# A hybrid encoder layer on one core: the skip product and the addition of the backward direction move from the vector engine to GpSimd in the forward SSM scan

## The chip, the cores and the metric

The kernel runs on one NeuronCore of one Trainium2 chip. The metric is the device time of one execution in microseconds (us), the median of several runs. TensorE is written PE, the vector engine DVE, the scalar engine ACT, GpSimd POOL, and the engine that issues most DMAs SP.

## The reference

One encoder layer on two request groups of 1024 and 256 tokens, in float32. A joint input projection feeds windowed attention, a bidirectional state-space scan (SSM) and attention to memory tokens; an output projection and a gated feed-forward part follow. The change lies in the SSM alone:

```
def ssd_bidirectional(z, xbc, dt_raw, conv_w, conv_b, dt_bias, a_log, d_skip, norm_w):
    ...
    y_f = ssd_scan(xs, dt[:, :, 0], a_neg[0], bm, cm)
    y_b = ssd_scan(xs[:, ::-1], dt[:, ::-1, 1], a_neg[1], bm[:, ::-1], cm[:, ::-1])[:, ::-1]
    y = y_f + y_b + d_skip.astype(jnp.float32)[:, None] * xs.astype(jnp.float32)
    y = y.reshape(b, s, SSM_INNER) * jax.nn.silu(z.astype(jnp.float32))
    return rms_norm(y, norm_w).astype(z.dtype)
```

The skip product is `d_skip * xs`; the addition of the backward direction is `+ y_b`.

## The kernel before

The program is a row of stages, each with a loop of its own per engine: norm, projections, the backward scan, the forward scan (`ssm_forward`), attention, memory attention, output projection, feed-forward. Engines meet at the end of each stage.

`ssm_backward` leaves, in the SBUF buffer `y_back`, the part of the backward direction that comes from the chunks behind. `ssm_forward` then goes through ten tiles of 128 tokens (t = 0 to 7 for the long sequence, 8 and 9 for the short one; the scan state is set to zero anew before tile 8). Each engine runs its own instruction list in order, and the lists meet through counting semaphores (`wait_ge`). In tile t:

- PE turns x and B of the tile (`x_ps`, `m_ps`), multiplies C by the state (`y_ps`), makes C·B (`m_ps`), then does 32 small matmuls (16 calls, each in two passes) for the tile before (`within(t-1)`, into `g_ps`, L1629), then the state update (`s_ps`) and the turning back of tile t-2.
- ACT copies `b_tok` and `x_tok` out of PSUM (L1747, L1748), makes the decay factors `drop` in two halves of eight small activations (L1758) and an exponential (L1764), squares the result of tile t-1 between the second half and its exponential (`squares`, L1727), and stores tile t-2.
- POOL multiplies `x_tok` by the step sizes into `x_dt` (two instructions, L1710), which it may overwrite only when `g_ps` of t-1 is finished (semaphore `diag`); then `mse` and `rstd` of tile t-1 (L1698, L1703).
- DVE copies `acs_t` (L1803), which ACT's factors wait for, makes `x_dec` (L1807), takes `y` out of PSUM (L1815), makes the skip product in `y2` (L1819), masks C·B (L1826, two instructions), adds `y_back` to `y2` (L1830), scales the state (L1834), adds `y2` to `y` (L1837), then gates tile t-1 (`gate`: L1786 adds `g_ps`, L1789 multiplies by z), updates the state (L1842), makes `m_t` from the factors (L1848, two instructions) and normalises tile t-1 (L1796), which waits for `rstd`.

In the profile's rows the buffer `y2` is shown as `sf_y`. The loop that PE waits in is closed like this: `within` of tile t-1 ends, DVE gates t-1, ACT squares it and, after its exponential, copies `b_tok` of the next tile, and only then PE goes on to C·B and to `within` of the next tile.

Of the kernel before, what the change touches and what calls it, by code (L numbers as in the profile page):

```python
# [1517 lines left out]
def ssm_forward(nc, proj, xbc_c, acs_rows, ident_dram, small, R, mix_t):  # L1518
# [6 lines left out]
    with ExitStack() as ctx:  # L1525
# [31 lines left out]
        g_ps = b.ps("sf_gps", [P, NS, PS])  # L1557
        t_ps = b.ps("sf_tps", [P, 4, P])
        S = {n: b.sem(f"sf_s_{n}") for n in (
            "const", "half", "turn", "xcopy", "bcopy", "xd", "off", "st", "h", "zero", "cb", "cbm", "acs", "drop", "e", "m", "diag", "y", "gated", "sq", "pow", "yn", "tn", "tcopy", "xdt")}  # L1560
        loaded, z_loaded, rows_loaded = b.sems("sf_l", 2), b.sems("sf_zl", 2), b.sems("sf_rl", 2)
        stored = b.sem("sf_stored")
        block = b.block()
# [16 lines left out]
        def before(t, n):  # L1580

            return isinstance(t, int) and t < n
# [32 lines left out]
        @block.tensor  # L1615
        def _(pe):
            T = nc.tensor
            pe.wait_ge(S["const"], 48)

            def within(t, first=False):  # L1620

                pe.wait_ge(S["xdt"], 2 * t + 2)
                pe.wait_ge(S["m"], 2 * t + 2)
                if not first:

                    pe.wait_ge(S["gated"], 2 * t - 1)
                for h in range(NS):
                    for d in range(2):
                        m = T.matmul(g_ps[:, h], m_t[:, d, h], x_dt[:, d, h], start=(d == 0), stop=(d == 1))  # L1629
                m.then_inc(S["diag"], 1)  # L1630

            def turn_back(t, s, first=False):
                pe.wait_ge(S["yn"], t + 1)
                if not first:
                    pe.wait_ge(S["tcopy"], t)
                for c in range(4):
                    m = T.transpose(t_ps[:, c], yn[:, s, c * P:(c + 1) * P], ident[:, :])
                m.then_inc(S["tn"], 1)

            def body(t, s):  # L1640
                first = before(t, 1)
                pe.wait_ge(loaded[s], loaded_value(t, s))
                if not first:

                    pe.wait_ge(S["xcopy"], t)
                    pe.wait_ge(S["bcopy"], t)
                    pe.wait_ge(S["cbm"], 2 * t)
                for c in range(4):
                    T.transpose(x_ps[:, 2 * c:2 * c + 2], xc[:, s, c * P:(c + 1) * P], ident[:, :])
                for g in range(NG):  # L1650
                    m = T.transpose(m_ps[:, g], xc[:, s, (4 + g) * P:(5 + g) * P], ident[:, :])
                m.then_inc(S["turn"], 1)

                if first:
                    pe.wait_ge(S["zero"], 1)
                else:
                    pe.wait_ge(S["h"], 2 * t)
                    pe.wait_ge(S["y"], 4 * t - 3)
                for g in range(NG):
                    m = T.matmul(y_ps[:, 4 * g:4 * g + 4], xc[:, s, (6 + g) * P:(7 + g) * P],  # L1660
                                 state[:, 4 * g:4 * g + 4], start=True, stop=True)
                m.then_inc(S["off"], 1)

                pe.wait_ge(S["bcopy"], t + 1)
                for g in range(NG):
                    m = T.matmul(m_ps[:, 2 + g], xc[:, s, (4 + g) * P:(5 + g) * P],
                                 xc[:, s, (6 + g) * P:(7 + g) * P], start=True, stop=True)
                m.then_inc(S["cb"], 1)
                if not first:
                    within(t - 1, before(t, 2))  # L1670
                pe.wait_ge(S["xd"], t + 1)
                for g in range(NG):
                    m = T.matmul(s_ps[:, 4 * g:4 * g + 4], b_tok[:, g], x_dec[:, 4 * g:4 * g + 4],
                                 start=True, stop=True)
                m.then_inc(S["st"], 1)
                if not before(t, 2):
                    turn_back(t - 2, s, before(t, 3))

            def reset(k):
                if k:  # L1680
                    pe.wait_ge(S["zero"], 2)

            order(pe, body, reset)
            within(NT - 1)
            turn_back(NT - 2, 0)
            turn_back(NT - 1, 1)

        @block.gpsimd
        def _(pool):
            b.clear_previous(pool)  # L1690
            g = nc.gpsimd
            g.memset(half[:, :], -0.5).then_inc(S["half"], 1)
            g.memset(eps[:, :], EPS).then_inc(S["half"], 1)
            pool.wait_ge(S["half"], 2)

            def rstd_of(t, first=False):
                pool.wait_ge(S["sq"], t + 1)
                g.tensor_tensor(mse[:, :], ms[:, :], eps[:, :], ALU.add).then_inc(S["pow"], 1)  # L1698
                pool.wait_ge(S["pow"], 2 * t + 1)
                if not first:  # L1700

                    pool.wait_ge(S["yn"], t)
                g.tensor_tensor(rstd[:, :], mse[:, :], half[:, :], ALU.pow).then_inc(S["pow"], 1)  # L1703

            def body(t, s):
                pool.wait_ge(S["xcopy"], t + 1)
                for d in range(2):
                    if not before(t, 1):
                        pool.wait_ge(S["diag"], t)
                    g.tensor_tensor(x_dt[:, d], x_tok[:, :, :], bc(row(dt, t, d * NS, (d + 1) * NS), [P, NS, PS]),  # L1710
                                    ALU.mult).then_inc(S["xdt"], 1)
                if not before(t, 1):
                    rstd_of(t - 1, before(t, 2))

            order(pool, body)
            rstd_of(NT - 1)

        @block.scalar
        def _(act):
# [19 lines left out]
            def body(t, s):  # L1739
                act.wait_ge(S["turn"], t + 1)  # L1740
                if not before(t, 1):
                    act.wait_ge(S["st"], t)

                    act.wait_ge(S["y"], 4 * t - 2)
                    act.wait_ge(S["xdt"], 2 * t)
                    act.wait_ge(S["xd"], t)
                a.activation(b_tok[:, :, :], m_ps[:, 0:2], ACT.Copy).then_inc(S["bcopy"], 1)  # L1747
                a.activation(x_tok[:, :, :], x_ps[:, :, :], ACT.Copy).then_inc(S["xcopy"], 1)  # L1748


                act.wait_ge(S["acs"], t + 1)
                for d in range(2):
                    if d == 0:
                        act.wait_ge(rows_loaded[s], loaded_value(t, s))
                    if not before(t, 1):
                        act.wait_ge(S["m"], 2 * t - 1 + d)
                    for h in range(NS):
                        m = a.activation(drop[:, d, h], rows[:, s, d, h], ACT.Relu, scale=-1.0,  # L1758
                                         bias=acs_t[:, s, d * NS + h:d * NS + h + 1])
                    m.then_inc(S["drop"], 1)  # L1760
                    if d == 1 and not before(t, 1):
                        squares(t - 1, 1 - s, before(t, 2))
                    act.wait_ge(S["drop"], 2 * t + d + 1)
                    a.activation(drop[:, d], drop[:, d], ACT.Exp, scale=-1.0).then_inc(S["e"], 1)  # L1764
                if not before(t, 2):
                    store(t - 2, before(t, 3))
# [8 lines left out]
        def _(dve):  # L1775
# [3 lines left out]
            def hp(ap):  # L1779
                return ap.rearrange("p (h q) -> p h q", q=PS)  # L1780

            def gate(t, s):

                dve.wait_ge(S["diag"], t + 1)
                dve.wait_ge(S["y"], 4 * t + 4)
                v.tensor_tensor(hp(y[:, s]), hp(y[:, s]), g_ps[:, :, :], ALU.add).then_inc(S["gated"], 1)  # L1786
                dve.wait_ge(S["gated"], 2 * t + 1)
                dve.wait_ge(z_loaded[s], loaded_value(t, s))
# [10 lines left out]
            def body(t, s):  # L1799
# [11 lines left out]
                if not before(t, 2):  # L1811
# [2 lines left out]
                    dve.wait_ge(S["yn"], t - 1)  # L1814
                v.tensor_tensor(hp(y[:, s]), y_ps[:, :, :], bc(row(e_acs, t, 0, NS), [P, NS, PS]),  # L1815
                                ALU.mult).then_inc(S["y"], 1)
                if not before(t, 1):
                    dve.wait_ge(S["y"], 4 * t)
                v.tensor_tensor(hp(y2[:, :]), x_tok[:, :, :], bc(dsk[:, :].unsqueeze(2), [P, NS, PS]),  # L1819
                                ALU.mult).then_inc(S["y"], 1)  # L1820

                dve.wait_ge(S["cb"], t + 1)
                if not before(t, 1):
# [1 line left out]
                for d in range(2):  # L1825
                    v.tensor_tensor(cb[:, d, :, 0], m_ps[:, 2:4], bc(tri[:, d:d + 1, :], [P, NG, P]),  # L1826
                                    ALU.mult).then_inc(S["cbm"], 1)
                dve.wait_ge(S["y"], 4 * t + 2)
                yb = y_back[:, t] if isinstance(t, int) else y_back[:, ds(t, 1)].rearrange("p o n -> p (o n)")
                v.tensor_tensor(y2[:, :], y2[:, :], yb, ALU.add).then_inc(S["y"], 1)  # L1830

                if not before(t, 1):
                    dve.wait_ge(S["h"], 2 * t)
                v.tensor_tensor(scaled[:, :, :], state[:, :, :], bc(row(e_tot, t, 0, NS), [P, NS, PS]),  # L1834
                                ALU.mult).then_inc(S["h"], 1)
                dve.wait_ge(S["y"], 4 * t + 3)
                v.tensor_tensor(y[:, s], y[:, s], y2[:, :], ALU.add).then_inc(S["y"], 1)  # L1837
                if not before(t, 1):
                    gate(t - 1, 1 - s)
# [679 lines left out]
```

## Time and profile before

| | us |
|---|---|
| median of 3 runs (lowest to highest) | 2209.69 (2207.54 to 2212.36) |
| the profiled execution, its own time | 2212.37 |
| its span, first to last instruction | 2210.6 |
| the forward scan, about 551 to 690 of the span | 139 |

The profiled execution is 2.7 us above the median, inside the spread of the runs. The forward scan is 6% of the span. In its rows, times are counted from the start of the span; a DVE row's length includes the tail that overlaps the next instruction, so that what an instruction costs its queue is the distance between two starts. "[idle before <- releaser]" stands behind an instruction whose engine sat idle before it.

### The profile page before, as it was taken

What the parts mean: (1) busy time and instruction counts of PE and PEld (TensorE: products, weight loads), DVE (VectorE), ACT (ScalarE), POOL (GpSimd) and SP (SyncE); (2) the same over time, 40 slices, a digit from 0 to 9 for tenths busy, and PEclk for the clock granted to TensorE, in tenths of its full rate; (3) what the DMA queues carried; (4) which work ended last, traced back from release to release, by engine and by line L of the source; (5) the groups of instructions that cost most, each with busy time, mean ns of one, the idle gap of its engine ahead of it and who ended that gap; (6) DMA issues with size and microseconds to landing.
All of it is one profiled execution on the core that took longest, in us unless ns stands there. A gap on an engine that the chain in (4) does not pass through costs nothing. (4 is left out here: it accounts for less than half of the span.)

```text
span 2210.6 us, 30145 instructions
## 1 busy us (share of the span) xinstructions
PE 2035.6 (92%) x10642; PEld 1735.0 (78%) x10642; DVE 1365.7 (62%) x1936; ACT 608.4 (28%) x1172; POOL 232.3 (11%) x242
## 2 busy tenths in 40 slices
PE   4999999996774999886999889999999999999997
PEld 3887888884674999875788778888888888888885
DVE  6664686235773888754423546766766766766766
ACT  5111121110673666641102321121121121121120
POOL 2000584040342100000000000000000000000000
PEclk7999999998776999988999999999999999999998
DMA  5323223213543111134511031010010010121002
GB/s 172 108 83 119 86 100 105 81 43 116 197 163 128 39 49 39 43 108 145 210 43 43 21 106 30 29 57 29 28 57 29 28 56 29 28 56 29 28 9 95
DMA packets 111118, 164.05 MB, mean 74 GB/s; under 512 B 8736, under 2 KB 68160, under 8 KB 109760
## 3 DMA queue, kind: packets, MB, share of 16 engines
q1 hardware_dynamic: 81648, 118.98, 16.8%
q10 hardware_dynamic: 29392, 44.07, 5.7%
q8 instruction: 45, 0.74, 0.1%
q14 instruction: 33, 0.27, 0.0%
HBM read 125.45 MB, written 37.57 MB: 74 GB/s over the span
## 5 line engine op out<-in xcount | busy, mean ns | idle before, releaser
L2398 PE MATMUL ff_proj<-h_hi,ff_uhi 128*128 128x512 f32 (+1 forms) x1056 | 374.5, 355 | 11.0 <-DVE ff_ulo L2311 11.0
L2398 PE MATMUL ff_proj<-h_lo,ff_uhi 128*128 128x512 f32 (+1 forms) x1056 | 374.3, 354 | 0.0
L2398 PE MATMUL ff_proj<-h_hi,ff_ulo 128*128 128x512 f32 (+1 forms) x1056 | 373.9, 354 | 0.0
L2357 DVE TENSOR_TENSOR x<-x,ff_proj 128x512 f32<-128x512 f32 x264 | 181.6, 688 | 185.3 <-PE ff_proj L2418 183.0
L2398 PEld LDWEIGHTS ff_proj<-h_hi,ff_uhi 128*128 128x128 f32 x1056 | 200.0, 189 | 40.1 <-DVE ff_ulo L2311 11.4
L2398 PEld LDWEIGHTS ff_proj<-h_lo,ff_uhi 128*128 128x128 f32 x1056 | 200.1, 189 | 28.6
L2398 PEld LDWEIGHTS ff_proj<-h_hi,ff_ulo 128*128 128x128 f32 x1056 | 199.9, 189 | 27.9
L576 PE MATMUL pj_bank<-pj_whi,act_hi 128*128 128x512 f32 x400 | 155.7, 389 | 0.0
L576 PE MATMUL pj_bank<-pj_whi,act_lo 128*128 128x512 f32 x400 | 155.6, 389 | 0.0
L576 PE MATMUL pj_bank<-pj_wlo,act_hi 128*128 128x512 f32 x400 | 155.6, 389 | 0.0
L2269 ACT ACTIVATE ff_padded<-ff_proj 128x1024 f32<-128x1024 f32 x44 | 45.3, 1028 | 350.4 <-PE ff_proj L2398 350.4
L2281 ACT ACTIVATE ff_ahi<-ff_gate 128x1281 fp32r<-128x1281 f32 x22 | 28.1, 1279 | 379.8 <-DVE ff_gate L2346 379.8
L2357 DVE TENSOR_TENSOR x<-x,ff_sums 128x512 f32<-128x512 f32 x176 | 121.1, 688 | 2.0 <-PE ff_sums L2418 0.3
L1065 PEld LDWEIGHTS at_ops<-at_v,at_pt 128*128 128x128 f32 x832 | 112.3, 192 | 2.5 <-DVE at_pt L979 2.0
L2418 PE MATMUL ff_proj<-ff_dhi,ff_ahi 128*128 128x512 f32 x264 | 104.9, 397 | 9.2 <-DVE ff_alo L2348 9.2
L1065 PE MATMUL at_ops<-at_v,at_pt 128*128 128x64 f32 (+1 forms) x832 | 111.8, 267 | 1.0 <-DVE at_pt L979 0.9
L925 ACT ACTIVATE at_pr<-at_sm,at_nm 128x385 f32<-128x385 f32 (+1 forms) x160 | 91.9, 575 | 72.6 <-DVE at_nm L996 56.0
L996 DVE CUSTOM_DVE_ANT_0 at_sm<-at_sps,at_mask,at_nsink 128x384 f32<-128x384 f32 (+1 forms) x160 | 89.9, 563 | 28.7 <-PE at_sps L1081 19.0
L2418 PE MATMUL ff_proj<-ff_dhi,ff_alo 128*128 128x512 f32 x264 | 104.9, 397 | 0.0
L2418 PE MATMUL ff_proj<-ff_dlo,ff_ahi 128*128 128x512 f32 x264 | 104.7, 396 | 0.0
L482 DVE TENSOR_REDUCE pj_dtraw<-hd_pieces 128x8 f32<-128x512 f32 (+2 forms) x44 | 27.3, 620 | 99.5 <-ACT hd_pieces L715 99.5
L641 POOL TENSOR_TENSOR hd_pieces<-hd_pieces 128x512 f32<-128x512 f32 (+1 forms) x44 | 57.6, 1310 | 290.9 <-DMA hd_pieces<-k_norm_w 179.0
(267 smaller groups left out, 4219.9 us busy)
## 6 DMA issues: line engine op xcount, KB each, us to landing
ff_rawu<-w_up SPq DMA_DIRECT2D x44, 512.0 KB, 4.9
pj_raw<-w_in SPq DMA_DIRECT2D x28, 512.0 KB, 3.7
ff_rawd<-w_down SPq DMA_DIRECT2D x22, 512.0 KB, 3.5
sf_rows<-scratch_acs_rows SPq DMA_DIRECT2D x10, 1024.0 KB, 7.6
wo_raw<-w_out SPq DMA_DIRECT2D x16, 512.0 KB, 4.3
scratch_proj<-hd_pieces ACTq DMA_DIRECT2D x30, 256.0 KB, 2.1
n_x<-tokens SPq DMA_DIRECT2D x14, 512.0 KB, 4.3
wo_mix<-scratch_mix ACTq DMA_DIRECT2D x9, 640.0 KB, 3.9
```

The costliest lines, as they stand in the source:

```text
L482: v.reduce_sum(ss[e % 2][:, 0:h], heads_of(h_sq[e % 2][:, 0:h * d], d), AX.X).then_inc(reduced, 1)
L576: m = nc.tensor.matmul(out, left(a, k), right(c, k), start=(k == 0 and i == 0), stop=(k == KC - 1 and i == 2))
L641: p_.tensor_tensor(heads_of(h_c[e % 2][:, 0:h * d], d), heads_of(h_raw[e % 3][:, 0:h * d], d), bc(w, [P, h, d]), ALU.mult).then_inc(weight ...
L925: nc.scalar.activation(pr[:, h % 4, 0:w], sm[:, h, 0:w], ACT.Exp, bias=nm[:, s, h:h + 1], scale=-1.0, accum_out=rowsum[:, s, h:h + 1]).the ...
L996: v.tensor_tensor_reduce(out=sm[:, h, 1:1 + w], in0=s_ps[:, h % 2, 0:w], in1=mask[:, k0 * P:k0 * P + w], scale=-(DH ** -0.5), scalar=nsink ...
L1065: m = T.matmul(o_ps[:, h], pt[:, h % 2, k - k0], rhs, start=(k == k0), stop=(k == k1 - 1))
L2269: nc.scalar.activation(padded[:, 1:1 + SEQ], proj[:, g, 0:SEQ], ACT.Copy)
L2281: nc.scalar.activation(a_hi[:, 1:GAP + 1 + DEC], gate[:, 1:GAP + 1 + DEC], ACT.Copy).then_inc(a_hi_done, 1)
L2357: nc.vector.tensor_tensor(v, v, ring(g), ALU.add).then_inc(added, 1)
L2398: m = nc.tensor.matmul(proj[:, g, t0:t0 + n], U[w][:, s, k, g], X[x][:, k, t0:t0 + n], start=(k == 0 and r == 0), stop=(k == KC - 1 and r ...
L2418: m = nc.tensor.matmul(ring(g), a[:, c0:c0 + P], w[:, s, cols], start=(r == 0), stop=(r == 2))
```

## The change

The skip product and the addition of `y_back` leave DVE's list and stand in POOL's, ahead of the two `x_dt` products, with a semaphore of their own (`skip`). DVE still adds `y2` to `y`, and now waits for POOL's second operation before it. POOL's product waits for `x_tok` and for DVE's last addition of `y2` (tile t-1); ACT, before it overwrites `x_tok`, waits for POOL's product and no longer for DVE's. The semaphore `y` now counts two per tile and not four.

```diff
@@ PE
-                    pe.wait_ge(S["y"], 4 * t - 3)
+                    pe.wait_ge(S["y"], 2 * t - 1)
@@ POOL
+            pool.wait_ge(S["const"], 48)
...
             def body(t, s):
                 pool.wait_ge(S["xcopy"], t + 1)
+                if not before(t, 1):
+                    pool.wait_ge(S["y"], 2 * t)
+                g.tensor_tensor(y2[:, :].rearrange("p (h q) -> p h q", q=PS), x_tok[:, :, :],
+                                bc(dsk[:, :].unsqueeze(2), [P, NS, PS]), ALU.mult).then_inc(S["skip"], 1)
+                yb = y_back[:, t] if isinstance(t, int) else y_back[:, ds(t, 1)].rearrange("p o n -> p (o n)")
+                pool.wait_ge(S["skip"], 2 * t + 1)
+                g.tensor_tensor(y2[:, :], y2[:, :], yb, ALU.add).then_inc(S["skip"], 1)
                 for d in range(2):
@@ ACT
-                    act.wait_ge(S["y"], 4 * t - 2)
+                    act.wait_ge(S["skip"], 2 * t - 1)
@@ DVE
-                dve.wait_ge(S["y"], 4 * t + 4)
+                dve.wait_ge(S["y"], 2 * t + 2)
...
-                if not before(t, 1):
-                    dve.wait_ge(S["y"], 4 * t)
-                v.tensor_tensor(hp(y2[:, :]), x_tok[:, :, :], bc(dsk[:, :].unsqueeze(2), [P, NS, PS]),
-                                ALU.mult).then_inc(S["y"], 1)
...
-                dve.wait_ge(S["y"], 4 * t + 2)
-                yb = y_back[:, t] if isinstance(t, int) else y_back[:, ds(t, 1)].rearrange("p o n -> p (o n)")
-                v.tensor_tensor(y2[:, :], y2[:, :], yb, ALU.add).then_inc(S["y"], 1)
...
-                dve.wait_ge(S["y"], 4 * t + 3)
+                dve.wait_ge(S["y"], 2 * t + 1)
+                dve.wait_ge(S["skip"], 2 * t + 2)
                 v.tensor_tensor(y[:, s], y[:, s], y2[:, :], ALU.add).then_inc(S["y"], 1)
```

DVE's list for tile 1, which stands written out ahead of the loop, was this (the operations and operands are named as in the list above):

```order
L1803 COPY sf_acst<-ss_acs 128x16
L1807 TENSOR_TENSOR sf_xdec<-sf_xtok,ss_dec 128x512
L1815 TENSOR_TENSOR sf_y<-sf_yps,ss_e_acs 128x512
L1819 TENSOR_TENSOR sf_y<-sf_xtok,sf_dskip 128x512
L1826 TENSOR_TENSOR sf_cb<-sf_mps,ss_tri 128x256 x2
L1830 TENSOR_TENSOR sf_y<-sf_y,ss_yback 128x512
L1834 TENSOR_TENSOR sf_scaled<-sf_state,ss_e_tot 128x512
L1837 TENSOR_TENSOR sf_y<-sf_y 128x512
L1786 TENSOR_TENSOR sf_y<-sf_y,sf_gps 128x512
```

and with the change, up to the same first instruction of the gate:

```order
L1811 COPY sf_acst<-ss_acs 128x16
L1815 TENSOR_TENSOR sf_xdec<-sf_xtok,ss_dec 128x512
L1823 TENSOR_TENSOR sf_y<-sf_yps,ss_e_acs 128x512
L1830 TENSOR_TENSOR sf_cb<-sf_mps,ss_tri 128x256 x2
L1835 TENSOR_TENSOR sf_scaled<-sf_state,ss_e_tot 128x512
L1839 TENSOR_TENSOR sf_y<-sf_y 128x512
L1794 TENSOR_TENSOR sf_y<-sf_y,sf_gps 128x512
```

The two operations of `y2` are gone, and everything behind them keeps its order. POOL's list for the same tile, ahead of the loop, is with the change:

```order
L1710 TENSOR_TENSOR sf_y<-sf_xtok,sf_dskip 128x512
L1714 TENSOR_TENSOR sf_y<-sf_y,ss_yback 128x512
L1718 TENSOR_TENSOR sf_xdt<-sf_xtok,ss_dt 128x512 x2
L1699 TENSOR_TENSOR sf_mse<-sf_ms,sf_eps 128x1
L1704 TENSOR_TENSOR sf_rstd<-sf_mse,sf_half 128x1
```

Before, the first two rows were not there; the others were the same and stood in the same order.

## Rows read from the trace of the kernel before

**Rows 1.** The page: busy time of each engine, share of the span, instructions.

```profile
PE 2035.6 (92%) x10642; PEld 1735.0 (78%) x10642; DVE 1365.7 (62%) x1936; ACT 608.4 (28%) x1172; POOL 232.3 (11%) x242
```

**Rows 2.** Busy time by stretch: the whole forward scan (PEclk is the granted clock).

```profile
551.00:690.00 139.00, 101.28 (x540) 90.79 (x540) 98.34 (x152) 89.58 (x231) 51.71 (x42) 0.74 0.45 154
```

**Rows 3.** Who waited for whom, 556 to 690: total us, times, longest.

```profile
POOL sf_xdt L1710 <- PE sf_gps L1629: 64.2, 9, 13.8
ACT sf_sq L1727 <- DVE sf_y L1789: 21.7, 6, 9.5
DVE sf_y L1786 <- PE sf_gps L1629: 17.4, 6, 6.0
...
DVE sf_yn L1796 <- POOL sf_rstd L1703: 5.7, 10, 1.7
...
ACT sf_drop L1758 <- DVE sf_acst L1803: 5.3, 8, 2.1
```

**Rows 4.** Timeline of DVE in tile 4: start us, length us, instruction.

```profile
605.29 0.69 DVE L1807 TENSOR_TENSOR sf_xdec<-sf_xtok,ss_dec 128x512 f32<-128x512 f32 x1
...
607.76 0.68 DVE L1830 TENSOR_TENSOR sf_y<-sf_y,ss_yback 128x512 f32<-128x512 f32 x1
...
608.96 0.68 DVE L1837 TENSOR_TENSOR sf_y<-sf_y 128x512 f32<-128x512 f32 x1
609.57 0.68 DVE L1786 TENSOR_TENSOR sf_y<-sf_y,sf_gps 128x512 f32<-128x512 f32 x1
610.39 0.70 DVE L1789 TENSOR_TENSOR sf_y<-sf_y,sf_z 128x512 f32<-128x512 f32 x1
```

**Rows 5.** Timeline of ACT in tile 4.

```profile
604.51 0.59 ACT L1748 ACTIVATE sf_xtok<-sf_xps 128x512 f32<-128x512 f32 x1
...
608.83 2.43 ACT L1758 ACTIVATE sf_drop<-sf_rows,sf_acst 128x128 f32<-128x128 f32 x8
611.26 0.63 ACT L1727 ACTIVATE sf_sq<-sf_y 128x512 f32<-128x512 f32 x1
```

**Rows 6.** Timeline of PE: the `within` matmuls during tiles 4 and 5.

```profile
605.22 3.68 PE L1629 MATMUL sf_gps<-sf_xdt,sf_mt 128*128 128x64 f32 x32
...
615.30 5.94 PE L1629 MATMUL sf_gps<-sf_xdt,sf_mt 128*128 128x64 f32 x32
```

**Rows 7.** Timeline of POOL around tile 4.

```profile
602.89 1.42 POOL L1703 TENSOR_TENSOR sf_rstd<-sf_mse,sf_half 128x1 f32<-128x1 f32 x1
609.16 2.84 POOL L1710 TENSOR_TENSOR sf_xdt<-sf_xtok,ss_dt 128x512 f32<-128x512 f32 x2 [4.85 <-PE sf_gps L1629]
```

**Rows 8.** Timeline of DVE in tile 5, at the gate.

```profile
621.37 0.69 DVE L1786 TENSOR_TENSOR sf_y<-sf_y,sf_gps 128x512 f32<-128x512 f32 x1 [1.61 <-PE sf_gps L1629]
622.19 0.88 DVE L1789 TENSOR_TENSOR sf_y<-sf_y,sf_z 128x512 f32<-128x512 f32 x1
```

**Rows 9.** Timeline of POOL: single instructions in tiles 3 and 5 and at the end.

```profile
601.64 1.17 POOL L1698 TENSOR_TENSOR sf_mse<-sf_ms,sf_eps 128x1 f32<-128x1 f32 x1
...
621.49 1.04 POOL L1710 TENSOR_TENSOR sf_xdt<-sf_xtok,ss_dt 128x512 f32<-128x512 f32 x1 [6.86 <-PE sf_gps L1629]
...
684.52 0.19 POOL L1698 TENSOR_TENSOR sf_mse<-sf_ms,sf_eps 128x1 f32<-128x1 f32 x1 [9.04 <-ACT sf_sq L1727]
684.79 0.55 POOL L1703 TENSOR_TENSOR sf_rstd<-sf_mse,sf_half 128x1 f32<-128x1 f32 x1
```

**Rows 10.** DVE's groups, 556 to 690: busy us, mean ns | idle before.

```profile
L1830 DVE TENSOR_TENSOR sf_y<-sf_y,ss_yback 128x512 f32<-128x512 f32 x10 | 7.0, 699 | 0.0
...
L1819 DVE TENSOR_TENSOR sf_y<-sf_xtok,sf_dskip 128x512 f32<-128x512 f32 x10 | 6.9, 686 | 0.0
```

**Rows 11.** The tile `sf_xdt`: POOL's instructions, ns least/median/most.

```profile
L1710 POOL TENSOR_TENSOR sf_xdt<-sf_xtok,ss_dt x20: 1042/1487/2181, 559.4 to 671.4; 128x512 f32<-128x512 f32 x20
```

**Rows 12.** Busy time by stretch: tile 3 and tile 4 (columns as in Rows 2).

```profile
592.00:605.00 13.00, 12.07 (x57) 11.16 (x56) 9.89 (x16) 8.90 (x24) 5.04 (x4) 0.61 0.50 169
605.00:615.00 10.00, 7.28 (x56) 6.45 (x55) 9.31 (x16) 8.78 (x24) 5.33 (x4) 1.00 0.64 196
```

More of the change, by code:

```diff
@@ L1559, in ssm_forward @@
         S = {n: b.sem(f"sf_s_{n}") for n in (
-            "const", "half", "turn", "xcopy", "bcopy", "xd", "off", "st", "h", "zero", "cb", "cbm", "acs", "drop", "e", "m", "diag", "y", "gated", "sq", "pow", "yn", "tn", "tcopy", "xdt")}
+            "const", "half", "skip", "turn", "xcopy", "bcopy", "xd", "off", "st", "h", "zero", "cb", "cbm", "acs", "drop", "e", "m", "diag", "y", "gated", "sq", "pow", "yn", "tn", "tcopy", "xdt")}
         loaded, z_loaded, rows_loaded = b.sems("sf_l", 2), b.sems("sf_zl", 2), b.sems("sf_rl", 2)
```

## The prediction, made before the changed kernel was run

> **What bounds the kernel now.** Start with the page: PE is busy for 92% of the span, DVE for 62%, POOL for 11% [rows 1]. But a share is a mean over stages, and the change touches one stage only, so the next view is the busy time of that stage alone. In the 139 us of the forward scan PE is busy 101 us, DVE 98, ACT 90 and POOL 52, at a mean granted clock of 0.74 [rows 2]. No engine is full, and DVE, PE and ACT are close together: who sets the pace has to be read from the waits. POOL stands idle for 64.2 us before its `x_dt` products until PE's `within` matmuls free the buffer, nine times; DVE stands idle for 17.4 us before the gate, six times, for the same matmuls; ACT stands idle six times, 21.7 us, before the square, until DVE has gated [rows 3]. So in six of the ten gates DVE is there early and PE is late, and ACT then waits through DVE for PE. The other four gates fall in tiles 2, 4, 6 and 9, and there the timelines have to be read.
>
> Tile 4 is one of them. PE's 32 matmuls take 3.68 us there and end at 605.22 + 3.68 = 608.90 [rows 6], but DVE reaches the gate only at 609.57, with no idle time ahead of it [rows 4]: here DVE is behind PE. The second step of the gate ends at 610.39 + 0.70 = 611.09. Yet ACT, which wants that result, is busy with its factors until 608.83 + 2.43 = 611.26, and takes the square at 611.26 without waiting [rows 5]. So DVE's lateness in this tile costs nothing: 0.17 us are left. Tiles 2, 6 and 9 repeat the pattern. Tile 5 is of the other kind: the same matmuls take 5.94 us [rows 6] and DVE idles 1.61 us before the gate [rows 8]. The two kinds differ by the clock that PE is granted: 1.00 (the 2.4 GHz level) over tile 4, 0.61 on the mean (mostly the 1.2 GHz level) over tile 3 [rows 12].
>
> In short: in six gates PE sets the pace, in four ACT. DVE's saved time lands in slack in both.
>
> **What it removes.** Two DVE instructions per tile, 0.69 and 0.70 us long [rows 10]. What one costs the queue is the distance between starts, 609.57 - 608.96 = 0.61 [rows 4], so 0.60 us each, 1.2 us per tile and 12.0 us over ten tiles. This is all that the change can give back directly.
>
> **What it adds.** Two POOL instructions per tile of the same shape as `x_dt`. Those took 1.04 us at the least, 1.49 in the median, 2.18 at the most [rows 11]. The spread has a visible cause: POOL's `mse` of one column takes 0.19 us at the end, where DVE is idle, and 1.17 us at 601.64, where DVE multiplies `m_t` from two SBUF operands; `rstd` takes 0.55 alone [rows 9] and 1.42 beside it [rows 7]. The other way round, DVE's product with z took 0.88 us at 622.19 while POOL was at work [rows 8], against 0.70 [rows 4]. DVE's first gate step, which has one operand in PSUM, took 0.68 to 0.69 us although POOL was at work too [rows 4, 8]. So POOL's work and DVE's instructions with two SBUF operands take turns, and each loses the other's time; those that read PSUM don't.
>
> The Trainium skill, "SBUF — State Buffer", section "Who interferes with whom", states just this: a DVE instruction with two SBUF inputs and a GpSimd instruction that reads SBUF hold a shared read port in turn, and the loser blocks fully. By that rule the two operations that DVE gives up come back to it as waiting. The trace agrees (0.19 against 1.17 us); by the rule DVE keeps about 0.25 us of the 1.2 in a tile like 4, without it all 1.2, and neither reaches ACT.
>
> **Tile 4 worked through.** `x_tok` is ready at 604.51 + 0.59 = 605.10 [rows 5]; POOL has been idle since 602.89 + 1.42 = 604.31 [rows 7]. It can start the product at about 605.2; DVE's `x_dec` starts at 605.29 [rows 4]. Which comes first is open, so both orders, at 1.04 us for an uncontended POOL instruction and 0.1 us for its semaphore:
> - DVE first: product 605.98 to 607.02, addition 607.1 to 608.14. DVE takes `y` and the two masks from PSUM meanwhile; it is through with the masks at 607.76 now [rows 4] and then, without the skip product ahead of them, at 607.16. The scaling of the state, next, has two SBUF operands and waits until 608.14. Then 0.60 each: the addition of `y2` at 608.74, the gate at 609.34.
> - POOL first: product 605.2 to 606.24, `x_dec` at 606.24, POOL's addition 606.9 to 607.94, DVE's masks done at 608.10, scaling, addition, gate at 609.30.
>
> Either way the gate comes 0.2 to 0.3 us earlier than 609.57, and still later than the matmuls' end at 608.90 and 0.13 us of signal (621.37 - 621.24, the end in [rows 6] to the start in [rows 8]). ACT does not see it, since it is free at 611.26. POOL is done at 608.14 at the latest, ahead of 609.16, where it starts `x_dt` now [rows 7]; so `x_dt`, `mse` and `rstd`, which now stand behind the two new instructions in POOL's queue, and DVE's normalisation, which waits for `rstd`, keep their times. What hides POOL's work is its 4.85 us of idle time here [rows 7] and 6.86 in tile 5 [rows 9]; if that cover were gone, every microsecond would go through `rstd`, the normalisation and `acs_t` to ACT.
>
> In the six others DVE idles 17.4 us in all before the gate [rows 3], 1.61 in tile 5 [rows 8]; that swallows what the turns cost, and PE's end does not move. The replaced semaphores (PE's, ACT's) have long been met in both cases, and one more semaphore to clear in a later stage lies ahead of a DMA wait.
>
> **Sum.** 2212.37 (the profiled execution) - 0.0 in six gates - 0.0 in four = 2212.4 for it; the median of the runs is 2.7 below, so 2209.5 as a median.
>
> **Bounds.** Downwards: ACT waits 5.3 us in all for `acs_t`, eight times, which DVE copies after the normalisation; most of that hangs on `rstd` (DVE itself waits 5.7 us for it) [rows 3]. If all of it went, 2209.7 - 5.3 = 2204.4. Upwards: if each new POOL instruction takes 2.18 us [rows 11], the second ends at 605.2 + 4.36 + 0.1 = 609.66; DVE's addition starts there, the gate 0.61 us later at 610.27, its product 0.82 us behind and 0.70 long ends at 611.79, and ACT is 0.53 us late: 2.1 us in the four tiles, 2211.8; with the run-to-run spread (2207.5 to 2212.4) to 2213.5. For the sum I take 1.04, since in the new place DVE reads PSUM for three of its instructions.
>
> **Rivals.** A measurement of this kernel tells a difference from none at about 0.2%, 4.4 us.
> 1. *DVE sets the pace after all.* For it: it is busy 98 of 139 us, and 9.3 to 9.9 us of each tile [rows 12]. Against it: ACT takes the square at 611.26 and not at 611.09. It would give 12.0 us: 2197.7. If only the four tiles gained the 0.54 us between 609.03 and 609.57, 2.2 us, 2207.5, inside the range. Chance 0.05.
> 2. *POOL becomes the bound (slower).* Its two new instructions stand ahead of `x_dt`. From 605.2 to 609.16 there is room for two of 1.9 us; beyond this each tile of the fast kind loses twice the excess, because DVE's wait for `y2` and POOL's `rstd` both slip. At 2.6 us each (above any row), 4 x 1.4 = 5.6 us: 2215.3. In the slow kind there is room for 3 us each. Chance 0.06.
> 3. *The granted clock falls differently.* PE idles in the fast tiles and is full in the slow ones, and the clock goes back and forth between them [rows 12]. A fast tile that turns slow costs 2 to 3 us (the matmuls' 5.94 against 3.68 [rows 6], whole tiles of 13.0 against 10.0 [rows 12]), and the reverse gives that. DVE's 0.2 us shift PE's waits a little, but not their sum. Two tiles must flip to pass 4.4 us: about 2204.5 or 2214.9. Chance 0.05 each way.
>
> That leaves 0.79 for no change. Faster: 0.05 + 0.05 = 0.10; slower: 0.06 + 0.05 = 0.11. The range is 2204.4 to 2213.5: down to the lower bound, up to the upper bound and the spread.
>
> **What the profile of the changed kernel would show.** DVE's busy time in the stage lower by some 12 us at most, the two groups gone; POOL's higher by 21 us at least (20 x 1.04); its idle time before `x_dt` smaller by about as much. POOL's new instructions 1.0 to 1.9 us long; DVE's scaling of the state or `x_dec` longer than 0.69 us in the tiles of the fast kind. ACT's wait for the gate still about 21.7 us in six tiles, and the fast tiles still about 10 us. I am wrong if ACT takes the square earlier in the fast tiles, if DVE waits for POOL's `skip` beyond 609.0 in a tile like 4, if `x_dt` starts after PE's end by more than the 0.26 us of now, or if the granted clock changes sides in two tiles or more.

## The result

| | us |
|---|---|
| changed kernel, median of 22 runs (lowest to highest) | 2214.01 (2207.86 to 2219.75) |
| kernel before, median of 22 runs beside it | 2210.59 (2205.39 to 2214.76) |
| ratio, 95% interval | 1.0017 (1.0009 to 1.0024) |

The changed kernel is slower by about 3.5 us. That is less than the 0.2% that I had named as the bound of the measurable, but clear of its interval, and half a microsecond above the upper end of my range.

The two profiled executions do not show it as a whole: their spans are 2210.3 us after and 2210.6 before. The granted clock hides it: the later tiles of the two executions met stretches at either clock level in a different order. During tile 7 PE's 32 matmuls took 6.93 us before and 3.68 after.

The timeline of PE in the kernel before:

```profile
638.01 6.93 PE L1629 MATMUL sf_gps<-sf_xdt,sf_mt 128*128 128x64 f32 x32
```

and in the changed kernel:

```profile
641.80 3.68 PE L1629 MATMUL sf_gps<-sf_xdt,sf_mt 128*128 128x64 f32 x32
```

So spans and sums over the stage can't be compared here between single traces; parts of equal clock can. 

**Busy time and waits.** The busy time of the forward scan in the changed kernel (columns as in [rows 2]):

```profile
551.00:690.00 139.00, 98.84 (x540) 88.39 (x540) 98.42 (x133) 89.15 (x231) 74.40 (x62) 0.76 0.44 154
```

POOL went from 51.7 to 74.4 us. Its twenty new instructions take 27.9 us (13.6 and 14.3 by group), and its other work takes 5.2 us less than before. DVE executes twenty instructions fewer and is as busy as before, 98.4 against 98.3 us. The groups of DVE in the changed kernel, 556 to 690, say where most of the 13.9 us of the two removed groups [rows 10] went:

```profile
L1835 DVE TENSOR_TENSOR sf_scaled<-sf_state,ss_e_tot 128x512 f32<-128x512 f32 x10 | 11.2, 1116 | 0.0
...
L1839 DVE TENSOR_TENSOR sf_y<-sf_y 128x512 f32<-128x512 f32 x10 | 8.5, 848 | 0.0
L1804 DVE SCALAR_TENSOR_TENSOR sf_yn<-sf_y,sf_rstd,sf_wn 128x512 f32<-128x512 f32 x10 | 8.3, 828 | 4.8 <-POOL sf_rstd L1704 4.8
...
L1811 DVE COPY sf_acst<-ss_acs 128x16 f32 (+1 forms) x10 | 5.3, 533 | 0.1
```

The scaling of the state, the addition of `y2`, the normalisation and even the copy of 16 numbers per partition (0.17 us when left alone) are longer, because POOL is at work beside them. The waits, 551 to 700, answer to [rows 3]:

```profile
POOL sf_xdt L1718 <- PE sf_gps L1629: 21.8, 9, 4.6
POOL sf_y L1710 <- ACT sf_xtok L1756: 21.1, 9, 7.4
ACT sf_sq L1735 <- DVE sf_y L1797: 17.7, 6, 8.2
DVE sf_y L1794 <- PE sf_gps L1629: 15.9, 6, 4.7
...
ACT sf_drop L1766 <- DVE sf_acst L1811: 8.9, 6, 4.0
```

POOL's wait for PE ahead of `x_dt` shrank by 42.4 us, twice the 21 that I had forecast, because POOL now idles 21.1 us for `x_tok` ahead of its product. ACT's wait for `acs_t` grew from 5.3 to 8.9 us.

**Where the time went.** Up to tile 3 the granted clock differs little between the traces; from tile 4 on it wanders. So the place to compare is tiles 2 and 3, from ACT's copy of `b_tok` of tile 2 to that of tile 4. In the trace of before, ACT's timeline has these rows:

```profile
579.41 0.36 ACT L1747 ACTIVATE sf_btok<-sf_mps 128x256 f32<-128x256 f32 x1
579.67 0.59 ACT L1748 ACTIVATE sf_xtok<-sf_xps 128x512 f32<-128x512 f32 x1
582.40 2.45 ACT L1758 ACTIVATE sf_drop<-sf_rows,sf_acst 128x128 f32<-128x128 f32 x8 [2.14 <-DVE sf_acst L1803]
...
591.27 0.38 ACT L1747 ACTIVATE sf_btok<-sf_mps 128x256 f32<-128x256 f32 x1 [0.94 <-ACT sf_ot L1734]
...
604.23 0.38 ACT L1747 ACTIVATE sf_btok<-sf_mps 128x256 f32<-128x256 f32 x1 [1.26 <-issue]
```

and in the changed kernel:

```profile
580.26 0.36 ACT L1755 ACTIVATE sf_btok<-sf_mps 128x256 f32<-128x256 f32 x1
580.52 0.59 ACT L1756 ACTIVATE sf_xtok<-sf_xps 128x512 f32<-128x512 f32 x1
585.09 2.45 ACT L1766 ACTIVATE sf_drop<-sf_rows,sf_acst 128x128 f32<-128x128 f32 x8 [3.98 <-DVE sf_acst L1811]
...
593.89 0.39 ACT L1755 ACTIVATE sf_btok<-sf_mps 128x256 f32<-128x256 f32 x1 [0.88 <-ACT sf_ot L1742]
...
608.44 0.38 ACT L1755 ACTIVATE sf_btok<-sf_mps 128x256 f32<-128x256 f32 x1 [1.21 <-issue]
```

Tile 2 took 11.86 us before (579.41 to 591.27) and takes 13.63 (580.26 to 593.89); tile 3 took 12.96 and takes 14.55. Together 3.36 us, about the difference of the medians.

Not all of that is the change. In tile 3 PE's C·B and its 32 matmuls ran partly at the higher clock level in the trace of before. The timeline of PE before:

```profile
591.70 0.71 PE L1666 MATMUL sf_mps<-sf_xc 128*128 128x128 f32 x4 [1.93 <-ACT sf_btok L1747]
592.25 6.70 PE L1629 MATMUL sf_gps<-sf_xdt,sf_mt 128*128 128x64 f32 x32
```

and in the changed kernel:

```profile
594.33 1.23 PE L1666 MATMUL sf_mps<-sf_xc 128*128 128x128 f32 x4 [1.99 <-ACT sf_btok L1755]
595.35 6.93 PE L1629 MATMUL sf_gps<-sf_xdt,sf_mt 128*128 128x64 f32 x32
```

The control that comes below, the kernel before with one wait moved, had C·B at 1.22 us and the 32 matmuls at 6.93. ACT's timeline there gives 13.66 us for tile 3 (tile 2 took 11.85):

```profile
590.75 0.38 ACT L1747 ACTIVATE sf_btok<-sf_mps 128x256 f32<-128x256 f32 x1 [0.94 <-ACT sf_ot L1734]
...
604.41 0.38 ACT L1747 ACTIVATE sf_btok<-sf_mps 128x256 f32<-128x256 f32 x1 [1.26 <-issue]
```

So 0.70 us of the difference in tile 3 come from the clock and 0.89 from the change, and the two tiles lose 2.7 us to it. What tiles 4 to 9 add can't be read from single traces.

*Tile 2.* `x_tok` is copied at 580.52 + 0.59 = 581.11, while POOL is still at `rstd` of the tile before. The timeline of POOL in the changed kernel, tile 2 and, in the last row, tile 3:

```profile
580.78 1.42 POOL L1704 TENSOR_TENSOR sf_rstd<-sf_mse,sf_half 128x1 f32<-128x1 f32 x1
582.17 1.04 POOL L1710 TENSOR_TENSOR sf_y<-sf_xtok,sf_dskip 128x512 f32<-128x512 f32 x1
583.40 1.48 POOL L1714 TENSOR_TENSOR sf_y<-sf_y,ss_yback 128x512 f32<-128x512 f32 x1 [0.19 <-POOL sf_y L1710]
...
602.46 2.04 POOL L1718 TENSOR_TENSOR sf_xdt<-sf_xtok,ss_dt 128x512 f32<-128x512 f32 x2 [4.53 <-PE sf_gps L1629]
```

`rstd` ends at 582.20 and the product follows at once. DVE, which has waited for the same `rstd`, comes 0.06 us later:

```profile
582.23 1.53 DVE L1804 SCALAR_TENSOR_TENSOR sf_yn<-sf_y,sf_rstd,sf_wn 128x512 f32<-128x512 f32 x1 [0.45 <-POOL sf_rstd L1704]
583.68 1.24 DVE L1811 COPY sf_acst<-ss_acs 128x16 f32 x1
...
587.53 1.52 DVE L1839 TENSOR_TENSOR sf_y<-sf_y 128x512 f32<-128x512 f32 x1
588.98 0.68 DVE L1794 TENSOR_TENSOR sf_y<-sf_y,sf_gps 128x512 f32<-128x512 f32 x1
...
602.31 0.69 DVE L1794 TENSOR_TENSOR sf_y<-sf_y,sf_gps 128x512 f32<-128x512 f32 x1 [3.23 <-PE sf_gps L1629]
603.51 1.54 DVE L1797 TENSOR_TENSOR sf_y<-sf_y,sf_z 128x512 f32<-128x512 f32 x1 [0.51 <-DVE sf_y L1794]
```

The normalisation takes 1.53 us (0.75 before) because it waits out POOL's product, and the copy 1.24 because it waits out POOL's addition. ACT waits for that copy in this tile, 2.14 us before and 3.98 now: it starts its factors 4.83 us after its copy of `b_tok`, where it was 2.99, and these 1.84 us are about what the tile lost. In the kernel before the normalisation and the copy were:

```profile
581.37 0.75 DVE L1796 SCALAR_TENSOR_TENSOR sf_yn<-sf_y,sf_rstd,sf_wn 128x512 f32<-128x512 f32 x1 [0.45 <-POOL sf_rstd L1703]
582.04 0.17 DVE L1803 COPY sf_acst<-ss_acs 128x16 f32 x1
```

*Tile 3.* The gate's second step, the product with z, starts 1.20 us after the first (602.31 to 603.51); before it was 0.83 us (599.07 to 599.90; 0.82 in the tile of [rows 8]). By then POOL has just begun its second `x_dt` product: its two ran 602.46 to 604.50 without a gap, and the product with z waits until the end of the second, 1.54 us for 0.88. ACT's square waits for it.

### The profile page after: what moved, and what is told of

Read it like the earlier page. It is cut to its first block and busy times, and to the rows that moved or that the text cites. A ratio compares the mean times of both kernels' runs of the same rounds, so it can differ in the third digit from the quotient of the medians.

```text
span 2210.3 us, 30126 instructions
## 1 busy us (share of the span) xinstructions
PE 2034.7 (92%) x10642; PEld 1733.7 (78%) x10642; DVE 1365.7 (62%) x1916; ACT 608.1 (28%) x1172; POOL 255.4 (12%) x262
## 5 line engine op out<-in xcount | busy, mean ns | idle before, releaser
L482 DVE TENSOR_REDUCE pj_dtraw<-hd_pieces 128x8 f32<-128x512 f32 (+2 forms) x44 | 27.3, 620 | 98.4 <-ACT hd_pieces L715 98.4
```

Source lines behind the costliest of these rows:

```text
L482: v.reduce_sum(ss[e % 2][:, 0:h], heads_of(h_sq[e % 2][:, 0:h * d], d), AX.X).then_inc(reduced, 1)
```

## The experiments

Theory: POOL's new work takes DVE's turn at places on the path, at the normalisation and the copy behind it (first repair) and in the gate (second repair). Rivals: DVE is late in the fast tiles, as in my rival 2; or only the clock differs. Each kernel was timed 12 times (one 6, one 11) beside 29 to 35 of the kernel before on the same chip.

**The change once more.** The same kernel again, for a second trace.

> The changed kernel once more, for a second trace and its time beside the other three on one chip. Theory: 2 to 5 us above before; the copy of acs_t over 0.9 us in three to five tiles, ACT's wait for it 8 to 10 us.

Measured: 2214.84 us, 1.0018 (1.0009 to 1.0026). The second trace has a span of 2214.5 us, so 4.2 us lie between two executions of one program. What repeats are the places: the copy of `acs_t` takes over 1 us in tiles 1, 2, 5, 7 and 9, ACT's wait for it is 9.7 us, and the product with z takes 1.54 us in tile 3 and 1.58 in tile 5.

**POOL waits for the copy (two runs).**

```diff
                 pool.wait_ge(S["xcopy"], t + 1)
+                pool.wait_ge(S["acs"], t + 1)
```

> The changed kernel, but POOL's product of tile t also waits until DVE has copied acs_t of tile t, so that it can no longer run beside DVE's normalisation and that copy. Theory (POOL holds up the normalisation and the copy that ACT's factors wait for): the copy takes 0.17 us in every tile, ACT's wait for it falls from 8.9 us back to 5.3 or less, and the time returns to the kernel before, within 0.1%. Rival 1 (DVE is held at the scaling of the state and the addition of y2 and gates late in the fast tiles): these stay at 1.2 to 1.7 us and the time stays 0.15 to 0.2% above before. Rival 2 (the granted clock): no change of ACT's wait explains the time; it differs as the slow stretches do.

> The changed kernel with only the first repair again (POOL's product waits until acs_t is copied), since its interval was wide (0.03 to 0.25%). Theory: 0.05 to 0.12% above before, the product with z at 1.54 us in tile 3. Rival: as the changed kernel, 0.17%.

Measured: 1.0014 (1.0003 to 1.0025), then 1.0002 (0.9991 to 1.0013). The copy takes 0.16 to 0.18 us everywhere and ACT's wait for it fell to 4.8 us. In both traces tile 2 took 12.4 us (13.6 with the change), tile 3 still 14.55, with the product with z at 1.54. ACT's timeline in the first of them, for tile 2:

```profile
580.20 0.38 ACT L1756 ACTIVATE sf_btok<-sf_mps 128x256 f32<-128x256 f32 x1
...
592.61 0.39 ACT L1756 ACTIVATE sf_btok<-sf_mps 128x256 f32<-128x256 f32 x1 [0.88 <-ACT sf_ot L1743]
```

So the first repair gives back 1.2 us of tile 2 and leaves tile 3; the two times lie too far apart to show a gain or its size.

**POOL's work on top, and DVE's relief alone.** In the first, POOL does the two operations into a buffer that nobody reads while DVE keeps its own; in the second neither does them.

> The kernel before, with POOL doing the two operations a second time into a buffer that nobody reads, at the place where the change puts them; DVE keeps its own. It prices POOL's work alone. Theory: the copy of acs_t is held up in some tiles as with the change, and the time is 3.4 to 6 us above before. Rival 1: DVE has two more instructions to be held at, so more than the change: 5 to 9 us. Rival 2: within 2 us of before unless the slow stretches grow.

> The changed kernel without POOL's two operations: the skip product and the backward direction are left out, y2 is a constant zero that DVE adds. It prices the relief of DVE alone. Theory: the relief lies in slack, 0 to 2 us faster than before, ACT's wait for the gate still about 21 us. If DVE set the pace it would be 12 us faster.

Measured: 1.0054 (1.0041 to 1.0067), 11.4 us between the medians, and 1.0005 (0.9994 to 1.0015). The relief is worth nothing that can be measured: DVE is busy 88.8 us instead of 98.3 and waits longer for PE (23.9 us before the gate, eight times). POOL's work alone costs far more than I expected of either theory. The timeline of DVE in the kernel with POOL's work on top shows why, in the fast tile 4:

```profile
614.00 1.54 DVE L1839 TENSOR_TENSOR sf_y<-sf_y,ss_yback 128x512 f32<-128x512 f32 x1
615.47 1.53 DVE L1843 TENSOR_TENSOR sf_scaled<-sf_state,ss_e_tot 128x512 f32<-128x512 f32 x1
616.91 0.68 DVE L1846 TENSOR_TENSOR sf_y<-sf_y 128x512 f32<-128x512 f32 x1
```

One instruction after the other waits out one of POOL's, and the gate comes 3.75 us after PE's end (0.67 before). So the 12 us that DVE gave up were needed as slack for POOL's work: without them it costs 11.4 us, with them 3.5.

**The wait for z ahead of the gate, and both repairs together (two runs).**

```diff
                 dve.wait_ge(S["y"], 2 * t + 2)
+                dve.wait_ge(z_loaded[s], loaded_value(t, s))
                 v.tensor_tensor(hp(y[:, s]), hp(y[:, s]), g_ps[:, :, :], ALU.add).then_inc(S["gated"], 1)
                 dve.wait_ge(S["gated"], 2 * t + 1)
-                dve.wait_ge(z_loaded[s], loaded_value(t, s))
```

> The changed kernel, but DVE's wait for the z tile stands ahead of the first step of the gate and no longer between its two steps. In the traces of the changed kernel the product with z starts 0.95 to 1.2 us after the first step in the odd tiles (0.82 before) and in some of them misses its turn against POOL's second x_dt product: 1.54 us long for 0.88. Theory (the turn in the gate is a second part of the price, about 1 us for each product that misses it): the product starts 0.85 us after the first step and is under 0.95 us long, and the time is 1 to 2 us below the changed kernel, 0.05 to 0.12% above before. Rival (all of the price is the held copy of acs_t): no change, 0.16 to 0.18% above before.

> The changed kernel with both: POOL's product waits until acs_t is copied, and the wait for the z tile stands ahead of the gate. Theory (held copy and missed turn together are the price): the time of the kernel before, within 0.07%. Rival (something else, the masks and the scaling held in the fast tiles): still 0.1% or more above before.

> The changed kernel with both repairs again, for a second trace and beside its control. Theory: within 0.07% of before once more. If the first result was luck of the clock: 0.1 to 0.18% above.

> The kernel before with the wait for the z tile ahead of the gate: the control for the two runs that moved this wait in the changed kernel. Theory (there the move only gives back a turn that the change had lost): no difference here, within 0.08%, since the product with z did not miss its turn before. Rival (the moved wait is a gain of its own that covers the price): 0.1% or more faster than before.

Measured: 1.0014 (1.0005 to 1.0022) for this repair alone, which can't be told from the change (1.0017); 0.9999 (0.9989 to 1.0009) and 1.0001 (0.9989 to 1.0012) for both; 1.0001 (0.9988 to 1.0014) for the control, the kernel before with the moved wait. With both repairs the time is that of the kernel before, twice, to within 0.12%, and the control shows no gain of the moved wait on its own. The timeline of DVE in the second trace with both repairs, tile 3:

```profile
602.12 0.69 DVE L1796 TENSOR_TENSOR sf_y<-sf_y,sf_gps 128x512 f32<-128x512 f32 x1 [3.33 <-PE sf_gps L1629]
602.84 0.91 DVE L1798 TENSOR_TENSOR sf_y<-sf_y,sf_z 128x512 f32<-128x512 f32 x1
```

The product with z now starts 0.72 us after the first step and gets the turn between POOL's two. The z tile itself had not been late: with its wait ahead of the gate, the first step still comes 0.14 us after PE's end (601.98). ACT's copies of `b_tok` in that trace give 12.42 us for tile 2 and 13.54 for tile 3:

```profile
581.18 0.36 ACT L1756 ACTIVATE sf_btok<-sf_mps 128x256 f32<-128x256 f32 x1
...
593.60 0.38 ACT L1756 ACTIVATE sf_btok<-sf_mps 128x256 f32<-128x256 f32 x1 [0.88 <-ACT sf_ot L1743]
...
607.14 0.38 ACT L1756 ACTIVATE sf_btok<-sf_mps 128x256 f32<-128x256 f32 x1 [1.21 <-issue]
```

Tiles 2 and 3 together: 28.2 us in both traces of the change, 27.0 with the first repair, 27.2 with the second, 26.0 with both, 24.8 in the kernel before and 25.5 in its control. So each repair gives back about 1 us in the tile at which it aims, and the rest, 0.5 us against the control, is not visible in the time. (The 1.2 us against the kernel before hold the 0.7 us of clock in its tile 3.)

**Another instruction for the copy.** `v.tensor_copy` of `acs_t` becomes `v.reduce_max` over an axis of one element.

> The changed kernel with the copy of acs_t done as a maximum over an axis of one element, which reads one operand from SBUF as the copy does. Theory (it is the copy as an instruction that takes turns with POOL, besides those with two SBUF operands): the maximum takes under 0.3 us in every tile while POOL is at work, where the copy took 1.0 to 1.2; ACT's wait for it falls below 8 us, the normalisation is still held in tile 2; the time is 1 to 2 us below the changed kernel. Rival (DVE's queue is held by the instruction ahead, whatever the next one is): the maximum also takes 1.0 us.

Measured: 1.0021 (1.0009 to 1.0033). The view of the tile `sf_acst` (ns least/median/most) in the changed kernel and in this one:

```profile
L1811 DVE COPY sf_acst<-ss_acs x10: 168/175/1235, 557.2 to 666.4; 128x16 f32 x6, 128x16 f32<-128x16 f32 x4
```

```profile
L1811 DVE TENSOR_REDUCE sf_acst<-ss_acs x10: 154/162/170, 556.9 to 667.3; 128x16 f32 x6, 128x16 f32<-128x16 f32 x4
```

What I expected of the instruction came true, what I expected of the time did not. ACT's wait for `acs_t` is back at 5.2 us and the kernel is as slow as the change. The held copy, which I had taken for the main part of the price, costs nothing that can be measured: tile 2 still takes 13.40 us, with the normalisation at 1.52 us and the gate 3.15 us after PE's end (1.45 before), and tile 3 14.55. In tile 2 ACT starts its factors 1.07 us sooner than with the change, and then waits for the late gate, as its timeline shows:

```profile
590.47 0.63 ACT L1735 ACTIVATE sf_sq<-sf_y 128x512 f32<-128x512 f32 x1 [0.73 <-DVE sf_y L1797]
```

**The copy earlier.** DVE copies `acs_t` of tile t+1 ahead of the `m_t` products of tile t, in the kernel before and, with the second repair, in the changed one.

> The kernel before, with DVE copying acs_t of tile t+1 ahead of the m_t products of tile t and no longer behind the normalisation. If ACT's wait for that copy is on the path in the fast tiles and in tile 2, 2 to 4 us faster than before; if it is hidden by PE, the same within 0.1%.

> The changed kernel with the wait for the z tile ahead of the gate and with acs_t of the next tile copied ahead of the m_t products, so that the copy is done long before POOL's product starts; nothing holds POOL back. Theory: ACT's wait for acs_t is gone, the normalisation is still held in tile 2, and the time is that of before within 0.08%; a gain over before needs DVE or ACT on the path and is not expected, as with the earlier copy in the kernel before.

Measured: 1.0007 (0.9998 to 1.0015) and 1.0003 (0.9993 to 1.0014). ACT no longer waits for `acs_t` at all, and gains nothing: in the kernel before its wait for the gate grew from 21.7 to 27.4 us. The waits of that run:

```profile
ACT sf_sq L1727 <- DVE sf_y L1789: 27.4, 10, 9.4
```

The second of the two still has the normalisation held in tile 2 (1.53 us) and takes 27.0 us for tiles 2 and 3, yet its time can't be told from that of the kernel before. So the microsecond that the held normalisation costs is read from tile 2; no time shows it by itself.

No version beats the kernel before.

## Why the prediction was wrong

- *The relief of DVE lies in slack*: right. 1.0005 with neither operation done. My rival 1 (12 us faster) is out.
- *POOL's instructions*: right. 1.04 to 1.68 us long, 27.9 us in all, inside POOL's idle time; `x_dt` started at most 0.19 us after PE's end (0.26 before).
- *Tile 4*: right. The scaling was held (1.72 us), the gate came 0.44 us after PE's end instead of 0.67, and ACT took the square without waiting.
- *The step that failed* is the sentence that, with POOL's work inside its idle time, "DVE's normalisation, which waits for `rstd`, keep their times", and with it "Tiles 2, 6 and 9 repeat the pattern". I followed one tile, took `x_dec` for the first DVE instruction that the product could meet, and called the other tiles a repetition. In tile 2 `x_tok` is ready more than a microsecond ahead of the normalisation (in the trace of before at 580.26, against 581.37), and what POOL's product waits for has long come: it starts the moment `rstd` is done, which is the moment for which DVE's normalisation waits too. DVE loses the turn by 0.06 us, and the normalisation takes 1.53 us. In that tile ACT already waited 2.14 of its 5.3 us for `acs_t` (0.28 in tile 4), so the delay reaches ACT. I had used this wait for the lower bound alone and put it at nothing in the sum and in the upper bound.
- *The gate in the slow kind* was taken as fixed by PE's end, and DVE's idle time was to swallow "what the turns cost". But the gate's second step has two SBUF operands and shares its turn with `x_dt`. In the odd tiles 3, 5 and 7 of the changed kernel it starts 0.1 to 0.4 us later behind the first step than before; in tile 3 it missed the turn in all five traces that have the change and not the second repair, and cost about 1 us there.
- *The upper bound* (2.1 us, 0.53 in each of four fast tiles) followed another path: tile 2 alone lost 1.77 us, and tile 3, which was to lose nothing, 0.89 at equal clock.
- *The arithmetic* had two slips: 2212.37 less 2.7 is 2209.7 and not 2209.5, and the spread that it names reaches 2.7 us above the median, which gives 2214.5 and not 2213.5 for the upper end. The measured 2214.01 would have been inside that range by luck, with the same wrong step.
- *Rival 2* had the right sign with a mechanism that did not occur; *rival 3*, the clock, moved single executions (tile 7 took 16.70 us in the trace of before and 13.24 in that of the change), but the median does not need it: both repairs bring it back.

The Trainium skill, "SBUF — State Buffer", section "Who interferes with whom", also counts a `copy` among the instructions that can contend with GpSimd, and says that a `tensor_reduce` never does. The traces agree, 1.24 against 0.17 us at the most. I had used the section for the two-operand instructions only.

Open: how the price divides between the two repairs, since the intervals are as wide as the parts; what tiles 4 to 9 add; and why the product with z came 0.1 to 0.4 us later in the odd tiles. POOL's work on top of the kernel before does not bring that delay (0.83 us between the two steps), nor does the changed kernel without POOL's two operations (0.82 to 0.83). That the wait's place decides it is shown, not what in the queue takes the time.

## What to carry to other kernels

Work that is moved from DVE to POOL is not hidden by POOL's idle time: in these traces DVE's instructions with two SBUF operands (and copies) stood still while it ran, so look at each DVE instruction that can fall beside it, in every tile of the pipeline's start and not in one typical tile. If both engines wait for the same event, the new instruction on POOL and the old one on DVE start a race; give POOL a wait that lets DVE's critical instruction through first. And where the granted clock moves single traces by more than the effect, compare stretches at which it is equal.

## What was not expected of the hardware

- A DVE copy of 128x16 numbers took 1.0 to 1.24 us beside POOL's work and 0.17 alone; a maximum over one element took 0.15 to 0.17 beside it.
- A start later by 0.4 us cost about 1 us, since the product with z missed the handover between two POOL instructions (603.51, when POOL had begun at 603.46).
- The same POOL work cost 3.5 us where DVE had given up the two instructions, and 11.4 where it kept them.
